# Dilated attention on keys kept in residue order, with copied queries and masks added by the tensor engine; block 1's values 512 wide

## The reference, cut to what matters

```python
DILATED_PATTERNS = ((128, 1), (512, 4), (2048, 16))
def dilated_window_attn(q, k, v, window, dilation):       # positions regrouped by residue mod dilation
    o, lse = banded_window_attn(to_res(q), to_res(k), to_res(v), window // dilation)
def banded_window_attn(q, k, v, window_keys):             # blocks of 128 queries against own and previous block
    s = jnp.einsum('nbqhd,nbkhd->nbhqk', qb, kk) * (hd ** -0.5)
    s = jnp.where(valid, s, -jnp.inf)                     # 0 <= distance <= 128, keys before the start left out
    p = jnp.exp(s - m); den = jnp.sum(p, -1); lse = m + jnp.log(den)
    o = jnp.einsum('nbhqk,nbkhd->nbqhd', p / den, vv)
mix_w = softmax(stack(lses), axis=0); o = sum(mix_w[..., None] * stack(outs))
```

## Time and profile before

| | |
|---|---|
| median of 3 runs | 2494.66 us (2490.2 to 2504.28) |
| the profiled execution: its own time | 2501.91 us |
| its span, first to last instruction | 2500.4 us |
| mean granted TensorE clock | 0.960 |
| PE, PEld busy | 2271.0 us (91%), 2058.7 us (82%) |
| DVE, ACT, POOL busy | 1366.4, 822.2, 687.8 us |
| chain that ended last | PE 66%, DVE 10%, DMA 9%, issue 6%, POOL 4% |

### The profile page before, as it was taken

One profiled execution on the slowest core, in us unless ns is written; L12 is line 12 of the kernel. 1 busy time (PEld: TensorE's weight loads), 2 busy tenths in 40 slices (PEclk: granted clock), 3 DMA queues, 4 the chain that ended last, 5 costly groups with the idle time before them and its releaser, 6 DMA issues.

```text
span 2500.4 us, 42787 instructions
## 1 busy us (share of the span) xinstructions
PE 2271.0 (91%) x16422; PEld 2058.7 (82%) x16422; DVE 1366.4 (55%) x3442; ACT 822.2 (33%) x1918; POOL 687.8 (28%) x658
## 2 busy tenths in 40 slices
PE   6999999986886999599999999999698898996898
PEld 5988989985775887599888889889698898895776
DVE  6513968754896544752565532131486777785421
ACT  4411111111785000341122201011486676674111
POOL 0012111163322987001212121110105354653222
PEclk9999999998898999799999999999899999998999
DMA  4341320235652232322555522111767866864443
GB/s 153 97 115 60 99 90 24 68 100 161 177 120 101 85 110 102 134 82 81 177 181 174 167 77 68 51 64 47 184 147 181 191 166 163 194 185 154 151 141 108
DMA packets 283805, 308.23 MB, mean 123 GB/s; under 512 B 38113, under 2 KB 221281, under 8 KB 280145
## 3 DMA queue, kind: packets, MB, share of 16 engines
q1 hardware_dynamic: 281776, 299.46, 41.9%
q0 software_dynamic: 1680, 5.51, 0.7%
q10 hardware_dynamic: 144, 0.52, 0.1%
HBM read 186.95 MB, written 105.89 MB: 117 GB/s over the span
## 4 chain that ended last, share of the span: by engine, by line
PE 66%; DVE 10%; DMA 9%; issue 6%; POOL 4%; SPq 3%; ACT 2%; POOLq 0%; ACTq 0%; DVEq 0%
PE bank L165 52%; DVE bank L710 4%; DMA cm<-scr_part 4%; PE bank L1852 3%; PE bank L1853 3%; PE bank L1863 3%; DMA woR<-in_w_out 2%; PE bank L1881 2%; SPq L1972 1%; PE bank L364 1%; POOL wol L1218 1%; POOL yo L2130 1%; PE bank L1286 0%; DVE p2l L1924 0%; DMA w2r<-in_w_in 0%
## 5 line engine op out<-in xcount | busy, mean ns | idle before, releaser
L165 PE MATMUL bank<-w1h,xh 128*128 128x256 f32 (+1 forms) x896 | 257.0, 287 | 0.2
L165 PE MATMUL bank<-w1l,xh 128*128 128x256 f32 (+1 forms) x896 | 253.7, 283 | 0.0
L165 PE MATMUL bank<-w1h,xl 128*128 128x256 f32 (+1 forms) x896 | 253.5, 283 | 0.0
L165 PE MATMUL bank<-xl,w2h 128*128 128x512 f32 x640 | 249.0, 389 | 0.0
L165 PE MATMUL bank<-xh,w2h 128*128 128x512 f32 x640 | 249.0, 389 | 0.0
L165 PE MATMUL bank<-xh,w2l 128*128 128x512 f32 x640 | 249.0, 389 | 0.0
L165 PE MATMUL bank<-w2h,xh 128*128 128x256 f32 x768 | 219.0, 285 | 10.5 <-issue 9.4
L165 PE MATMUL bank<-w2l,xh 128*128 128x256 f32 x768 | 218.5, 285 | 0.0
L165 PE MATMUL bank<-w2h,xl 128*128 128x256 f32 x768 | 218.5, 284 | 0.0
L1918 DVE CUSTOM_DVE_ANT_0 s2m<-bank,mask 128x256 f32<-128x256 f32 (+1 forms) x576 | 185.9, 360 | 46.5 <-PE bank L1853 45.1
L1863 PE MATMUL bank<-ident,p2r 128*128 128x128 f32 x900 | 159.0, 290 | 42.5 <-DVE p2l L1924 42.1
(11 more groups left out here) (274 smaller groups left out, 5926.5 us busy)
## 6 DMA issues: line engine op xcount, KB each, us to landing
scr_part<-ob SPq DMA_DIRECT2D x48, 264.0 KB, 2.9
cm<-scr_part SPq DMA_DIRECT2D x48, 264.0 KB, 5.1
v<-scr_v SPq DMA_DIRECT2D x12, 1040.0 KB, 8.2
w2r<-in_w_in SPq DMA_DIRECT2D x12, 1024.0 KB, 6.6
qr<-qf SPq DMA_DIRECT2D x192, 64.0 KB, 2.0
ax<-in_x SPq DMA_DIRECT2D x16, 512.0 KB, 6.2
xr<-in_x SPq DMA_DIRECT2D x16, 512.0 KB, 4.6
bx<-scr_x SPq DMA_DIRECT2D x16, 512.0 KB, 6.7
```

The source lines that it names most:

```text
L165: ins = nc.tensor.matmul(dst, x, y, start=k == 0 and m == 0, stop=k == n - 1 and m == 2)
```

## The change

- Block 1: the values of a group are made like its keys, 24 matmuls with 512 columns, so they come out turned. ScalarE scales them into `vf`, TensorE turns them back (4 matmuls, work item `turn_v`, behind group 1 of the same rows), then ScalarE, VectorE and SyncE do as before.
- Rope stage: key tiles are split and stored with the 512 positions of a tile in order of their residue mod 16, 32 positions each. Queries stay in order.
- Dilated stage, keys: read in that order, so d = 16 and d = 4 read runs of 32 elements and d = 1 runs of 8. The values of d = 1 and d = 4 are loaded in the matching order, by 16 DMAs each (of 8 partitions for d = 1, of 32 for d = 4). The first values are issued by ScalarE.
- Queries for d > 1: GpSimd copies them for two units at a time (512 elements a partition, 96 copies in all) into one of six buffers, listed eight steps ahead of their use.
- One-block units: the mask is added by one more matmul (bf16 identity, 256 columns); VectorE takes one minimum over 2 x 128; ScalarE reads the scores from PSUM, and the bank comes free with the exponentials.
- Mixes of j < 5: three more steps between A and B, two more between B and G.

```diff
-        if kind == "f":
+        if kind in "fv":
             fs, ss = slice(128 * step, 128 * step + 128), slice(512 * g, 512 * g + 512)
             return products(bank[:], lambda k: (wh[:, k, fs], wl[:, k, fs]), lambda k: (xh[:, k, ss], xl[:, k, ss]), 8)
...
+                elif item[0] == "turn_v":
+                    g = item[1]
+                    bank, before = v_bank[g]
+                    pe.wait_ge(*a_vf.at(g + 1))
+                    pe.wait_ge(*before)
+                    for t in range(4):
+                        ins = nc.tensor.transpose(bank[:, 128 * t:128 * t + 128], vf[g % 2][:, 128 * t:128 * t + 128], ident[:])
+                    ins.then_inc(*p_vt.up())
...
-            nc.scalar.activation(hbuf[m % 2][:], qf[m % 3][:], ACT.Copy).then_inc(*a_qh.up())
+            nc.scalar.activation(stored(m, hbuf[m % 2]), taken(m, qf[m % 3]), ACT.Copy).then_inc(*a_qh.up())
...
-            mixing.append([t, [None] * delay + ["A"] + [None] * (3 if j < 5 else 0) + list("BCDEFG")])
+            mixing.append([t, [None] * delay + ["A"] + ([None] * 6 + ["B", None, "C", "D", None, "E", "F", "G"] if j < 5 else list("BCDEFG"))])
...
         def step(s):
+            if s + 8 in copies:
+                work.append(("queries", copies.index(s + 8)))
...
+        def keys_of(x, k):
+            d, r, b, nk = x["d"], x["r"], x["b"], x["nk"]
+            if d == 16:
+                return k[:].rearrange("p (g r a) -> p r g a", g=4, r=16)[:, r]
+            if d == 4:
+                return k[:].rearrange("p (g i r a) -> p r g i a", g=4, i=4, r=4)[:, r, b - nk + 1:b + 1]
+            at = [512 * (c // 4) + 8 * (c % 4) for c in (b - nk + 1, b)]
+            return bass.AP(k, at[0], [[S, 128], [at[1] - at[0], nk], [32, 16], [1, 8]] if nk > 1 else [[S, 128], [32, 16], [1, 8]])
...
+                if x["nk"] == 1:
+                    pe.wait_ge(*d_mask.at(9))
+                    nc.tensor.matmul(bank[:].rearrange("p (h k) -> p h k", h=2)[:, :, 0:128], unit16[:], own16[:, PATTERNS.index(d)], start=True, stop=False)
                 for hh in range(2):
                     dst = bank[:, 256 * hh:256 * hh + w]
-                    nc.tensor.matmul(dst, buf[hh][:, qc], buf[2 + hh][:, kc], start=True, stop=False)
-                    ins = nc.tensor.matmul(dst, buf[hh][:, qc], buf[4 + hh][:, kc], start=False, stop=True)
+                    qx = q[:, hh, 128 * b:128 * b + 128] if d == 1 else qs[x["copy"] % 6][:, hh, x["g"] % 2, :]
+                    nc.tensor.matmul(dst, qx, keys_of(x, buf[hh]), start=x["nk"] == 2, stop=False)
+                    ins = nc.tensor.matmul(dst, qx, keys_of(x, buf[2 + hh]), start=False, stop=x["nk"] == 2 or hh == 1)
...
+            k = 16 // d
+            view = v23.rearrange("(b a i r) c -> r i a b c", a=128 // k, i=k, r=d)
+            for r in range(d):
+                for i in range(k):
+                    rows = slice(128 // k * i, 128 // k * i + 128 // k)
+                    e.dma_start(vr[n % 2][rows, r * nb:r * nb + nb, :], view[r][i][:, :, c:c + 2 * VW]).then_inc(*v_in[n % 2].up(16))
...
+                if x["nk"] == 1:
+                    nc.vector.tensor_reduce(row[:, 130:132], x["s"][0][:].rearrange("p (h k) -> p h k", h=2)[:, :, 0:128],
+                                            mybir.AxisListType.X, ALU.min).then_inc(*d_mx.up())
+                    return
...
+                src = (qn[j % 2][:].rearrange("p h (b m r) -> p r h b m", b=4, r=4)[:, r, :, b:b + 2] if d == 4 else
+                       qn[j % 2][:].rearrange("p h (m r) -> p h r m", r=16)[:, :, r:r + 2])
+                nc.gpsimd.tensor_copy(qs[c % 6][:], src).then_inc(*g_qs.up())
```

More of the change, by code:

```diff
@@ L285, in norm_stage @@
                 work.append(("group", 1, g - 1))
+                if turned:
+                    work.append(("turn_v", g - 1))
             work.append(("group", 0, g))
-        work += [("load", 2), ("group", 1, 3), ("consts",), ("load", 3)]
+        work += [("load", 2), ("group", 1, 3)]
+        if turned:
+            work.append(("turn_v", 3))
+        work += [("consts",), ("load", 3)]
         work += [("group", 2, g) for g in range(4)]
         bk = Banks(range(8))
-        turn_bank, steps, n_mm, n_split, n_val = {}, {}, 0, 0, 0
+        turn_bank, v_bank, steps, n_mm, n_split, n_val = {}, {}, {}, 0, 0, 0
         for item in work:
@@ L305, in norm_stage @@
                         n_val += 1
-                        steps[n, g].append((kind, step, n_mm, n_val, bk.take(d_v.at(n_val))))
+                        steps[n, g].append((kind, step, n_mm, n_val, bk.take(a_vf.at(n_val) if kind == "v" else d_v.at(n_val))))
                 wts.spent[n] = p_mm.at(n_mm)
+            elif item[0] == "turn_v":
+                v_bank[item[1]] = bk.take(d_v.at(item[1] + 1))
         def sp_fetch(g):
@@ L1651, in dilated_stage @@
                 units.append(dict(n=n, j=j, d=d, g=g, r=r, b=b, nk=nk, w=128 * nk, v0=r * nb + b - nk + 1))
+        for u in range(N):
+            units[u]["min"] = (units[u - 1]["min"] if u else 0) + units[u]["nk"]
+        copies = [u for u in range(N) if units[u]["d"] > 1 and units[u]["g"] % 2 == 0]
+        for c, u in enumerate(copies):
+            units[u]["copy"] = units[u + 1]["copy"] = c
         work, later, mixing, n_mix = [], [], [], 0
@@ L1883, in pe_unit, with load_values @@
                 ins.then_inc(*p_o.up())
+        def load_values(e, n):
+            j, d = pairs[n]
+            nb, c = NT // d, 2 * VW * j
+            if d == 16:
+                e.dma_start(vr[n % 2][:], v23.rearrange("(p r) c -> p r c", r=16)[:, :, c:c + 2 * VW]).then_inc(*v_in[n % 2].up(16))
+                return
[5 more added lines that the diff above has]
+                    e.dma_start(vr[n % 2][rows, r * nb:r * nb + nb, :], view[r][i][:, :, c:c + 2 * VW]).then_inc(*v_in[n % 2].up(16))
         def act_unit(item):
-            if item[0] == "turn":
+            if item == ("values", 0):
+                load_values(nc.scalar, 0)
+            elif item[0] == "turn":
                 u, x = item[1], units[item[1]]
@@ L1950, in pool_unit @@
         def pool_unit(item):
-            if item[0] == "mix":
+            if item[0] == "queries":
+                c, x = item[1], units[copies[item[1]]]
+                j, d, r, b = x["j"], x["d"], x["r"], x["b"]
+                if j == 0:
+                    for i in range(4):
+                        pool.wait_ge(*q0_in[i].at(160))
+                else:
+                    pool.wait_ge(*qk_in[j % 2].at(160 * ((j + 1) // 2)))
+                pool.wait_ge(*g_zero.at(4))
+                if c >= 6:
+                    pool.wait_ge(*p_s.at(copies[c - 6] + 2))
+                src = (qn[j % 2][:].rearrange("p h (b m r) -> p r h b m", b=4, r=4)[:, r, :, b:b + 2] if d == 4 else
+                       qn[j % 2][:].rearrange("p h (m r) -> p h r m", r=16)[:, :, r:r + 2])
+                nc.gpsimd.tensor_copy(qs[c % 6][:], src).then_inc(*g_qs.up())
+            elif item[0] == "mix":
                 m = mixes[item[1]]
@@ L1969, in sp_unit @@
                 if part_ == 4:
[L1970 removed]
+                    nc.sync.dma_start(f(buf[2 + hh][own, cols]), k2l[rows, cols]).then_inc(*done.up(16))
                 elif part_ % 2 == 0:
[L1972 removed]
+                    nc.sync.dma_start(f(qn[j % 2][half, hh, cols]), (q2h, q2l)[hh ^ (part_ // 2)][rows, cols]).then_inc(*done.up(16))
                 else:
[L1974 to L1986 removed]
+                    nc.sync.dma_start(f(buf[hh][half, cols]), k2h[rows, cols]).then_inc(*done.up(16))
+            elif item[0] == "values" and item[1] > 0:
+                if item[1] >= 2:
+                    sp.wait_ge(*p_o.at(16 * (item[1] - 1)))
+                load_values(nc.sync, item[1])
             elif item[0] == "weights":
```

118 lines of the change are left out of this document (72 added, 46 removed).

## The result

The changed kernel takes 2516.8 us (median of 20 runs, 2505.92 to 2526.06), the kernel before 2501.68 us (20 runs, 2490.20 to 2510.68): ratio 1.0053, 95% interval 1.004 to 1.0067. The forecast was 2432, the range 2355 to 2480, and slower had 6 in 100. The profiled execution of the changed kernel took 2510.14 us by its own time (span 2508.3). Head pairs are counted from 0 where a number stands; "the fourth head pair" is number 3.

What follows compares the result with a forecast made beforehand. It took TensorE, level with ScalarE at d = 1, to bound the dilated units, and transfers to set head pairs 1 to 4. -20.8 - 22.8 - 13 - 6.5 = -63 from 2501.9 gave 2439 profiled, 2432 against the median; range 2355 to 2480.

Steps and rivals of the forecast that it cites:

- Block 1: Block 1's values as 512-column matmuls and an earlier load of chunk 2: -20.8 us, with what follows keeping its length.
- Scores and masks: Dilated stage: two-block units of d = 4 fall from 1.93 to 1.36 us, one-block units to 1.0; d = 1 stays.
- Query copies: GpSimd's 96 copies at 0.9 us, 14 us a head pair beside the mixes: cost 0, up to 2 a head pair.
- Transfers: Sixteen value issues of d = 4 add +2.5 us; third mix at +58.5; head pairs 1 to 4 -5.7 each, -22.8.
- The three extra steps are worth nothing there: the transfer is what is late: Third mix of a head pair: moving it from step 27 to 30 changes nothing, since its transfer comes later than the units.
- First head pair: It has no mixes: -7.9 - 6.3 us, +1 for masks and values sharing the start with queries: -13.
- Last head pair: -5 - 5.5 + 4 = -6.5 us; mixes ending five steps later are covered by the tail's weight loads.
- Values of d = 1: 16 DMAs of 8 partitions take 16 to 20 us: nothing lost in head pairs 1 to 4, +4 in the last.
- C: Rival: values of d = 1, loading in 22 to 26 us, hold the units at each head pair: about +35, 2467; chance 0.16.
- D: Rival: runs of 8 and 32 read no faster than strides, so d = 4 and 16 gain little: 2485; chance 0.07.
- E: Rival: values of d = 1 take 40 us, 24 late at each of five head pairs, +120: 2552; chance 0.06.
- B: Rival: the units set all head pairs, 59.5 us each, the wait being from the order of issues: 2352; chance 0.24.

Runs made afterwards that it cites:

- e1: Kernel before with only block 1's values made 512 columns wide, dilated stage as before: 2477.7 us, ratio 0.9896.
- e4: Changed kernel without the query copies, queries of d > 1 read by stride from the tile, keys still in runs: 2524.0 us, ratio 1.0083.
- e8: Changed kernel without query copies, queries of every unit read contiguous (scores of other rows, not the reference): 2514.3 us, ratio 1.0035.
- e14: Changed kernel with old mix distances, `cm` early, values by one and four DMAs in old order, no query copies; not the reference: 2428.2 us, ratio 0.9705.
- e3: Changed kernel with values of d = 1 by one DMA and d = 4 by four, in old row order (not the reference): 2483.6 us, ratio 0.9921.
- e2: Changed kernel with the old distances in the mixes (three steps between A and B, none between B and G): 2500.7 us, ratio 0.9983.
- e5: Changed kernel with old mix distances from B on and `cm` of second and third mix loaded early (steps 8 and 22): 2468.2 us, ratio 0.9844.
- e9: Kernel before with block 1's values 512 wide and `cm` of second and third mix early (steps 8 and 22): 2448.7 us, ratio 0.9789.
- e7: Changed kernel with old mix distances and values by one and four DMAs in old row order (not the reference): 2459.0 us, ratio 0.9813.
- e13: Changed kernel with old mix distances, `cm` early, values by one and four DMAs in old row order (not the reference): 2428.6 us, ratio 0.9722.

## Why the prediction was wrong

*Block 1* (-20.8): right, 22.1 by the profile and 24 to 25 by e1.

*Scores and masks*: the unit distances 1.36 and 1.0 came out as 1.36 and 0.93. Their reason was told of both operands alike, with "a moving operand in runs of 8" as the unknown; e4 shows that without contiguous queries, the stationary operand, 0.43 to 0.47 us a unit come back. The unknown cost nothing: units of d = 1 take 1.36 us with runs of 8, and took 1.35. What the keys' new order adds beside contiguous queries stays open.

*Query copies* (0): right. They take 1.09 us each where 0.9 was said, and e8 and e14 put them at 2.5 and 0.5 us in all, beside other waits that may hide more.

*Transfers*, "+3 to +7, part of it hidden by `cm` and `gt` under way: I take +2.5": mis-sized. The sixteen issues of d = 4 took 8.7 us, +5.8 over four, and all ten loads stand behind them. In head pair 1 the third mix did start at +58.7, where 58.5 was forecast, 2.1 later than before; in head pairs 2 to 4 at 61.4 to 62.7, 3.9 to 8.6 later. How much of that is the issues' is not settled: with four issues (e3) the third mix starts at 55.4 and 56.8 in head pairs 1 and 2, but at 62.2 and 62.6, no earlier, in 3 and 4, each of which still begins with a wait of 4 us for `kept`.

*"The three extra steps are worth nothing there: the transfer is what is late"*: this step failed. It is true of the third mix alone. Behind it the forecast put 20 us of units, and 27.6 to 29 were measured: the fourth mix's parts come to ScalarE while GpSimd is in the third, and its part G comes to the next head pair's start. In the fast units of d = 16, nine steps are 8.4 us, and a mix keeps GpSimd busy for 10.1 (a quarter of 40.3) and the copies between for 4 to 5 more. With the old distances the kernel is 16 us faster (e2). The second and the first mix, of which the prediction said nothing, are later too.

*First head pair* (-13) with "+1 for the masks and for values that share the start with the queries": mis-sized. From the rope stage to head pair 1 it came to +0.4. The units of the first head pair gave 8.6 of the 14.2 (81.4 to 72.8 us), and the first scores come 22.4 us behind the rope stage instead of 13.4, 9.0 back, where the term had +1. The sixteen DMAs of d = 1 take from 1739.2 to 1778.5; with one DMA in their place the start is 14.4 us shorter (e3).

*Last head pair* (-6.5) and "Mixes that end five steps later have the weight loads of the tail as cover": this step failed as well. From head pair 5 to the end it came to +8.2: 1.2 less up to the last scores and 9.3 more behind them. There was no cover, since the load of the last weights waits in SyncE's list for the mixes; with the old distances the 9.3 us are gone (e2).

*Values of d = 1* ("I take 16 to 20, nothing lost"): behind the start of the stage the 2048 packets are moved in 10.2 to 14.3 us (11.8 in the fourth head pair, from 2084.3), where one DMA of before took 4.1 at the same place: sooner than forecast. Only in head pair 1, where the last packets come at 1838.5, does TensorE stand for them, with units of 3.17, 2.12 and 2.21 us in place of three of about 1.4. At the start of the stage, beside the loads of queries and keys, they need 37.5. The 16 to 20 us were an estimate between the bounds of 3.4 and 40, and no run shows them: the measured 11.8 us for 1.06 MB are 90 GB/s, where 16 to 20 us would be 53 to 67.

*The rivals*: C came nearest in its cause (values of d = 1), though not in place: the price is SyncE's time and the start of the stage, not late values at each head pair. D was right that runs of 32 gain little by themselves (1.83 us for 1.93 in e4), but beside contiguous queries the units had their gain (1.36). E, the one on the slower side, did not happen. B needed the order of issues rather than the engines to be the limit; e5 and e9 show that this was half true: moving `cm` in SyncE's list alone gives 30 us in either dilated stage, though not B's 59.5 us a head pair.

The sum, by the runs: 2516.8 as changed; 58 less without the new distances and the sixteen-fold value DMAs (e7); 30 less with `cm` early (e13), 2428.6. The forecast of 2432 had the units' gain right, but put +1 on the start and +2.5 a head pair on the issues, nothing on the distances, and kept the wait for the third `cm`. That e13 comes out near 2432 is chance: it has lost that wait, which the forecast had in it. Against the forecast, by the profiles: head pairs 1 to 4 are 44 us off (+21.4 where -22.8 was said), the last and the tail 15, the first 13, block 1 -1. Taken alone, the dilated stage's change is worth +39 us against e1 (2516.8 - 2477.7), and -17 to -20 against e9 when nothing else stands in the way (e13, whose values are not in the keys' order). Open is what the start of the stage waits for in detail, and whether values stored in HBM in the keys' order, which would need few DMAs, bring e13's time with the right output: that was not tried.

## What to carry to other kernels

An engine that issues DMAs is an engine: count its issues in us and ask what is queued behind them. Here 6 us more of issues ahead of ten loads cost 2.4 us a head pair where other waits covered them (e3), 3.4 with the old distances (e7 against e2) and 7.2 where `cm` was early too (e13 against e5), with the same bytes. Look behind the stage as well: work that ends a few steps later can hold a load of the next stage. When units get faster, work that was spread over them by steps comes closer together in time: check each spread chain against the duration of its steps, at the fastest pattern. And before paying for a new order of data, find out which operand's stride it is that costs.

## What the runs showed of the hardware that had not been expected

- With queries by stride as the stationary operand, it hardly mattered how the moving keys were read: 1.93 us by stride and 1.83 in runs for a unit of d = 4. With the queries contiguous as well it was 1.36.
- SyncE's issue of a value DMA of 128 packets of 520 bytes took 0.32 us where it covered 8 partitions, 0.43 where it covered 32 and 0.60 where it covered 128, each the most frequent value of its kind; many in between other loads took longer. An issue of 512 packets over 128 partitions took 0.51.
- Behind the start of the stage, the changed kernel's packets of 520 bytes took 28 ns each (median of 2048) in each of the five sets of DMAs over 32 partitions, and 28 to 38 in the six DMAs over 128. In the five sets of sixteen DMAs over 8 partitions each that SyncE issues in the changed kernel the median was 62, 49, 51, 47 and 31 ns; what sets it was not tested.
